# Gated linear attention: weight loads issued one stage later, and the last modulation sums made on column strips inside the last head

## The reference, cut to what matters

```python
mod_lat = jnp.split(jax.nn.silu(c) @ w_mod[layer] + b_mod[layer], N_MOD, axis=-1)
sh1, sc1, g1, sh2, sc2, g2 = mod_lat
...
q = to_heads(parts[6], GLA_HEADS)           # 4 heads, key width 128, value width 256
k = to_heads(parts[7], GLA_HEADS)
v = to_heads(parts[8], GLA_HEADS)
g_f = gla_log_gate(lr[..., :GLA_GATE_RANK], w_f, b_f)
g_b = gla_log_gate(lr[..., GLA_GATE_RANK:], w_b, b_b)
...
x = x + g1 * y_lat
h = modulate(rms_norm(x, norm_ffn_g[layer]), sh2, sc2)
```

## Time and profile before

| | |
|---|---|
| median of 3 runs | 2749.3 us (2748.82 to 2750.38) |
| the profiled execution, its own time | 2749.08 us |
| the profiled execution, its span | 2747.3 us |
| mean granted TensorE clock | 0.947 of full speed |
| busy: PE, PEld, DVE, ACT, POOL | 2458.9, 1698.2, 1244.6, 873.0, 158.3 us |
| rank stage (first transfer issued to start of the head stage) | 505.87 to 530.64 us |
| head stage (start to start of the merge) | 530.64 to 748.50 us |

### The profile page before, as it was taken

One profiled execution on the slowest core, in us unless ns is written; L12 is line 12 of the kernel. 1 busy time (PEld: TensorE's weight loads), 2 busy tenths in 40 slices (PEclk: granted clock), 3 DMA queues, 4 the chain that ended last, 5 costly groups with the idle time before them and its releaser, 6 DMA issues. The chain is left out here.

```text
span 2747.3 us, 43114 instructions
## 1 busy us (share of the span) xinstructions
PE 2458.9 (90%) x17416; PEld 1698.2 (62%) x17417; DVE 1244.6 (45%) x2882; ACT 873.0 (32%) x1889; POOL 158.3 (6%) x177
## 2 busy tenths in 40 slices
PE   6789999599799999999899988987897999888998
PEld 4667777376598443333333333326777999867998
DVE  4457776388466111111111111115756565676664
ACT  4255454223253111111111111114335355335453
POOL 0333433000000000000000000000000000000000
PEclk8889998899799999999999999998888999988999
DMA  6521210543068999999999999995313556313553
GB/s 217 72 63 40 55 33 2 163 144 126 28 197 277 397 409 409 409 409 409 409 408 409 409 409 408 409 378 176 92 36 111 163 175 178 100 54 108 173 184 114
DMA packets 254674, 601.83 MB, mean 219 GB/s; under 512 B 26146, under 2 KB 82697, under 8 KB 253449
## 3 DMA queue, kind: packets, MB, share of 16 engines
q1 hardware_dynamic: 253388, 598.58, 60.9%
q10 hardware_dynamic: 1085, 0.45, 0.1%
HBM read 594.57 MB, written 4.39 MB: 218 GB/s over the span
## 5 line engine op out<-in xcount | busy, mean ns | idle before, releaser
L2499 PE MATMUL banks<-moe_raw,moe_xs 128*64 128x512 f32 x2048 | 474.6, 601 | 30.7 <-DMA moe_raw<-in_w_gu 29.4
L2964 PE MATMUL banks<-xs_r,w_hi 128*128 128x272 f32 (+1 forms) x1408 | 408.2, 290 | 23.1 <-DVE w_raw_r L3432 14.4
L2968 PE MATMUL banks<-xs_r,w_raw_r 128*128 128x272 f32 (+1 forms) x1408 | 406.6, 289 | 0.0
L2965 PE MATMUL banks<-xs_r,w_hi 128*128 128x272 f32 (+1 forms) x1408 | 405.1, 288 | 0.0
L2499 PEld LDWEIGHTS banks<-moe_raw,moe_xs 128*64 128x64 f32 x2048 | 134.4, 137 | 301.4 <-issue 222.3
L2448 DVE TENSOR_TENSOR gu<-banks,vec 128x512 f32<-128x512 f32 x64 | 44.3, 692 | 601.8 <-PE banks L2529 601.7
L3248 ACT ACTIVATE w_hi<-w_raw 128x512 fp32r<-128x512 f32 (+1 forms) x416 | 251.6, 617 | 201.6 <-PE banks L2968 163.5
L3432 DVE TENSOR_TENSOR w_raw_r<-w_raw,w_hi 128x512 fp32r<-128x512 f32 (+1 forms) x416 | 268.1, 677 | 68.4 <-ACT w_hi L3248 64.0
L2964 PEld LDWEIGHTS banks<-xs_r,w_hi 128*128 128x128 f32 x1408 | 268.3, 191 | 27.2 <-issue 24.8
L2499 PE MATMUL banks<-moe_raw,moe_act 128*64 128x512 f32 x1024 | 240.4, 599 | 40.2 <-DMA moe_raw<-in_w_down 38.6
L2968 PEld LDWEIGHTS banks<-xs_r,w_raw_r 128*128 128x128 f32 x1408 | 268.4, 191 | 2.2
(11 more groups left out here) (508 smaller groups left out, 4096.9 us busy)
## 6 DMA issues: line engine op xcount, KB each, us to landing
moe_raw<-in_w_gu SPq DMA_DIRECT2D x256, 1024.0 KB, 18.5
moe_raw<-in_w_down SPq DMA_DIRECT2D x128, 1024.0 KB, 18.6
w_raw<-in_w_ff SPq DMA_DIRECT2D x256, 256.0 KB, 3.0
w_raw<-in_w_in SPq DMA_DIRECT2D x112, 256.0 KB, 2.7
gdn_w<-in_w_in SPq DMA_DIRECT2D x32, 512.0 KB, 4.0
mod_ring<-in_w_mod SPq DMA_DIRECT2D x16, 1024.0 KB, 5.2
ring_mod<-in_w_mod SPq DMA_DIRECT2D x8, 1024.0 KB, 18.5
wh<-in_w_in SPq DMA_DIRECT2D x8, 1024.0 KB, 9.7
```

The costliest lines, as they stand in the source:

```text
L2499: ins = pe.matmul(out if ph == "d" else out.rearrange("p (j x) -> p j x", x=P), x[:, 2 * q + k, :], w[:, c * 512:(c + 1) * 512] if ph == " ...
L2964: pe.matmul(bank, w_hi, x[:, 0, 0:n_cols], start=first, stop=False)
L2965: pe.matmul(bank, w_hi, x[:, 1, 0:n_cols], start=False, stop=False)
L2968: ins = pe.matmul(bank, w_lo, x[:, 0, 0:n_cols], start=False, stop=last)
```

## The change

Two edits, both in `gla`. First, units 0 to 2 of the modulation and the weights of head 1 are no longer issued by SP in the rank stage but as the first thing in the head stage; `load_head(0)` stays where it is. Second, the 32 products behind the last head are taken away. In their place stand, in head 3, `late_sum` behind the updates of step 0 (8 products with a weight of 32 columns, each of which writes 512 columns to one of four strips in banks 6 and 7), two copies of a bank into slot 0 of `mod_ring` by DVE at step 1, `late_turn` behind the updates of step 3 (8 products of 4 columns), and DVE's addition of the bias at step 4. There is one more semaphore.

```diff
@@ rank stage, SP
                 load_head(sp, 0)
-                for u in range(3):
-                    load_mod(sp, u)
-                load_head(sp, 1)
@@ head stage, SP
+                for u in range(3):
+                    load_mod(sp, u)
+                load_head(sp, 1)
                 late(3, 4, 5)
@@ head stage, PE
+                def late_sum():
+                    pe.wait_ge(silu_a, 2 * GLA_H)
+                    pe.wait_ge(mod_v, 8 * KT)
+                    for g in range(8):
+                        ins = pe.matmul(ps[6 + g // 4][g % 4 * Q:(g % 4 + 1) * Q, :], ones[:, 0:Q], mod_sum[:, g, :], start=True, stop=True)
+                    ins.then_inc(mod_mm, 1)
+
+                def late_turn():
+                    pe.wait_ge(mod_sb, 2)
+                    for m in range(8):
+                        ins = pe.matmul(ps[6][:, 4 * m:4 * m + 4], mod_ring[:, 0, m // 4, m % 4 * P:(m % 4 + 1) * P],
+                                        ident.rearrange("p (g q) -> p g q", g=4)[:, :, 0], start=True, stop=True)
+                    ins.then_inc(mod_mm, 1)
...
                         if h + 1 < GLA_H:
                             project(h + 1, i)
+                        elif i == 0:
+                            late_sum()
+                        elif i == 3:
+                            late_turn()
                         if h and i == 2:
                             turned(h - 1)
...
                 turned(GLA_H - 1)
-                pe.wait_ge(mod_v, 8 * KT)
-                for m in range(4 * 8):
-                    ins = pe.matmul(ps[2][:, m:m + 1], mod_sum[:, m // 4, m % 4 * P:(m % 4 + 1) * P], ones[:, 0:1],
-                                    start=True, stop=True)
-                ins.then_inc(mod_mm, 1)
@@ head stage, DVE
                         if h + 1 < GLA_H:
                             decay(h + 1, i)
+                        elif i == 1:
+                            dve.wait_ge(mod_mm, 1)
+                            for n in range(2):
+                                dve.tensor_copy(mod_ring[:, 0, n, :], ps[6 + n][:, :]).then_inc(mod_sb, 1)
+                        elif i == 4:
+                            dve.wait_ge(mod_mm, 2)
+                            dve.tensor_tensor(modT[:, 2 * KT:6 * KT, 0].rearrange("p (n g m) -> p n g m", n=2, g=4),
+                                              ps[6][:, 0:32].rearrange("p (n m g) -> p n g m", n=2, m=4),
+                                              vec[:, V_BMOD + 2 * KT:V_BMOD + 6 * KT].rearrange("p (n g m) -> p n g m", n=2, g=4), ALU.add)
                 for part in range(4):
                     norm(GLA_H - 1, part)
-                dve.wait_ge(mod_mm, 1)
-                dve.tensor_tensor(modT[:, 2 * KT:6 * KT, 0], ps[2][:, 0:4 * KT], vec[:, V_BMOD + 2 * KT:V_BMOD + 6 * KT], ALU.add)
```

More of the change, by code:

```diff
@@ L1448, in gla @@
                        "gla_cum_v gla_vv gla_diff_v gla_e_v gla_kd_v gla_att_v gla_s0 gla_s1 gla_o_v gla_sq_a gla_var_v gla_inv_v "
-                       "gla_n_v gla_y_v gla_exp_a gla_ln_a gla_ex_a gla_silu_a gla_std_a gla_mod_v gla_mod_mm", held=loaded + mod_in) as \
+                       "gla_n_v gla_y_v gla_exp_a gla_ln_a gla_ex_a gla_silu_a gla_std_a gla_mod_v gla_mod_mm gla_mod_sb", held=loaded + mod_in) as \
                 (block, gate_mm, q_mm, k_mm, v_mm, rb_mm, gram_mm, tr_mm, up0, up1, o_mm, turn_mm,
@@ L1452, in gla @@
                  cum_v, v_v, diff_v, e_v, kd_v, att_v, s0, s1, o_v, sq_a, var_v, inv_v,
-                 n_v, y_v, exp_a, ln_a, ex_a, silu_a, std_a, mod_v, mod_mm):
+                 n_v, y_v, exp_a, ln_a, ex_a, silu_a, std_a, mod_v, mod_mm, mod_sb):
             ups, ss = (up0, up1), (s0, s1)
```

## The result

| | before | after |
|---|---|---|
| median, same chip, 4 runs each | 2749.84 us (2748.82 to 2755.70) | 2732.53 us (2727.70 to 2734.74) |
| the profiled execution, its own time | 2749.08 us | 2727.70 us |
| the profiled execution, its span | 2747.3 us | 2725.9 us |

The ratio is 0.9913, 95% interval 0.9894 to 0.9932: 0.87% faster, 18.7 to 29.1 us with 23.9 in the middle. The difference of the medians is 17.3 us, that of the profiled executions 21.4. The forecast was a gain of 24.0 us and a median of 2725.3 us, with 2719 to 2735 as the range; the measured median lies in it, 7.2 us above the forecast.

A forecast was written before the change was run, and what follows sets the result against it. PE was busy 90% of the span; SP's issues held the head stage's start and 32 PE products its end. Gains of 14.75 (12.75 + 2.0) and 9.3 us sum to 24.0: 2749.3 - 24.0 = 2725.3 us, range 2719 to 2735.

The forecast's parts named there:

- What held the start: Rank stage's end: SP's issuing held it to 529.30; without seven issues DVE ends it at 516.55, 12.75 us less.
- Transfers: Head stage: all weights land in time; rival: transfers share engines evenly, about 2 to 8 us lost, chance 0.08.
- The clock at the start: Start of the head stage: with less idling PE keeps 2.4 GHz longer, 2.0 us gained (0 to 3.1).
- The last head: Head 3 and behind it: 12.76 us removed, 3.5 us of added work, so 9.3 us gained.
- The middle: From 560 to 708: PE busy 147.25 of 148 us, so what is won before is passed through.
- the clock in part: Case given 0.03 jointly with a slower kernel; a low PE clock takes part of the gain.
- From the profiled execution to the median: Whole kernel: profiled execution 0.2 us from the median of the runs; 2749.3 less 24.0 gives 2725.3 us.
- The first edit without effect: Rival at the rank stage's end: something other than SP's issuing holds it, 12.75 us not gained, 2740.0 us; chance 0.05.
- The last head eating its gain: Rival in head 3: slow `late_turn`, low clock, serial strips; 3.6 to 6.4 us instead of 9.3; chance 0.12.
- Slower by a lasting low clock: Rival: the PE-bound stretch runs at 1.2 GHz, 2778 us if through the whole head stage; 0.03 jointly with partial clock loss.
- The price of the slow clock: PE-bound head stage: 0.28 us lost per us at 1.2 GHz; the 24 us gain gone after 86 us longer.
- Six groups of products: Last three steps of the last head: 0.65 to 1.24 us each, at most 3.0 us more, 0.1 taken.

The follow-up runs named there:

- e_front: The kernel before with the first edit alone, the 32 products behind the last head kept; median 2742.04 us, ratio 0.9940.
- e_mods: The changed kernel with head 1's weights issued in the rank stage again, only units 0 to 2 moved; 2738.71 us (one run), rank stage 16.75 us.
- e_late: The changed kernel with `late_turn` behind step 7 of the last head and the bias between norm parts 2 and 3; 2732.26 us, ratio 0.9909.
- e_best2: A repeat of e_best, run beside the changed kernel; median 2728.12 us, ratio 0.9888 to the kernel before.
- e_rows: The changed kernel with gate products on 128 rows (16 to 127 zeros) and gate weights loaded behind head 0's first two transfers; 2730.89 us, ratio 0.9898.
- e_best: The changed kernel with the edits of e_rows and e_late together; median 2728.57 us, ratio 0.9885 to the kernel before.
- e_rows_before: The kernel before with only gate products on 128 rows and gate weights loaded behind head 0's first two transfers; 2753.63 us, ratio 0.9986.

## Why the prediction was right, point by point

**What held the start.** Right. With the seven issues gone the rank stage ended with DVE; the head stage's first product came 1.24 us behind DVE's copy (taken: 1.38). The rank stage lost 13.15 us in the changed kernel and 13.13 in e_front (12.75 forecast). e_mods shows the same from the other side: SP last again, the stage longer again.

**Transfers.** Head 0 was called covered "with nothing to spare" at the faster clock; its last transfer landed 9.6 us after its issue, as long as before (9.7), and missed by 0.93 us of one weight load. PE also had to wait for the first half of `z`, which DVE had at about 518.54 (half of L1613's 1.61 us behind 517.79), so the transfer cost 0.2 us at most. Units 0 and 1 and head 1 held nobody up; unit 0 landed 5.2 us after its issue, at 521.8.

**The clock at the start.** 2.0 us were taken between 0 and 3.1. From the stage's start to the key product it was 8.69 us and is 7.29: 1.4. The guess that the gates would run at 2.4 GHz and the clock fall behind them was what happened.

**The last head.** 3.5 us were taken, 3.12 measured. `late_sum` took 1.92 (1.8), so the strips do run side by side; it begins 0.64 us behind the first record of step 0, with no gap that a drain would need. The turn came 7.00 us after step 0 and not 6.24, 0.8 later (0.9). `late_turn` took 3.57 (3.4), at 1.2 GHz as assumed. e_late took 1.94 of the 3.12 away, e_best2 all of it.

**The middle.** Here one step failed: that what is won at the start is simply passed through, with nobody waiting for the clock. In 148 us between the heads PE was busy for 147.25 us before and 147.26 after, and yet it took 3.4 us longer for the same work, as it was granted 1.2 GHz at two more places. The prediction looked at the clock where it expected idleness and took it as 1.00 in between, though the trace of before already held one such dip (L1484 at 663.63 with 5.37 us). The 0.03 for "the clock in part" was too little for it: of the nine profiles with 16-row gates four have none, two or three dips instead of one, so 1.7 us less to 3.4 us more belonged to the terms of the sum, beside those of the two ends.

**From the profiled execution to the median.** The forecast took the measured scatter, 1.6 us, for the kernel's. More runs of before gave 2747 to 2767 on another chip, and even in the first comparison the fourth was 2755.7. Of the 7.2 us between forecast and median, 2.4 are between forecast and the profiled execution: the dips 3.4 and the clock at the start 0.6 on the one side, on the other 0.4 each from the last head and the rank stage and some 0.9 from ahead of the rank stage, which the change does not touch. The other 4.8 are what the median lies above that execution. For those four runs no trace says where they stand; in the pair of profiles that differ in the same way it was PE's clock behind 1856. On the other chips, with more runs, the medians of before and changed lie 23.8 us (2756.53, 2732.73) and 22.6 us (2757.02, 2734.42) apart. That the first comparison shows only 17.3, and that its median still lies in the range, says little of the forecast: with four runs each, both are in part luck.

**The rivals.** Transfers: no. The first edit without effect: no, and e_mods, where SP's issues alone make the stage longer again, shows it from the other side. The Trainium skill says (Runtime: NRT & Kernel Launch, Instruction fetch mechanics) that a branch to a target which isn't loaded forces a fetch by DMA before the engine goes on. Nothing in this trace calls for such a wait: 1.24 us at that barrier, head 0's last bytes still under way, and 1.41 at the earlier trace rows. The last head eating its gain: no, 9.6 us remained. Slower by a lasting low clock: no, but its small relative, the dips, was there.

**Where its sums and readings were off.** None of these changes the forecast. The price of the slow clock was taken as 0.28 us for each us, from 5.17 against 3.72; but that product ran from 534.36 to 539.5 and the clock was back at 537.3, so 2.2 of its 5.17 us were already fast. A dip of 3.3 us costs 1.7, that is 0.5 for each: the gain would be gone after 48 us of such a clock and not 86, and the whole head stage at 1.2 GHz would give some 2820 us and not 2778. The clock of before fell at about 520.2 (0.56 in the window from 520) and not shortly after 521. Six groups of products that grow from 0.65 to 1.24 are 3.5 us and not 3.0. Unit 0 was called covered by 4.7 us with the slow start alone; at the faster one DVE asked at 525.09, 3.3 us after it had landed. And 387 GB/s is not about all that is seen: the profile page of the kernel before has slices with 409. What a drain at a change of tiling would cost no run shows; there is no idle stretch in front of `late_sum` or behind it.

## What to carry to other kernels

An engine that issues transfers behind others still under way (here 12.5 us for four, against 1.5 for three on an almost empty queue) holds a barrier as much as one that computes: issue behind the barrier what is needed behind it, and check only that the first user is covered. Where an engine is busy all through, look at its granted clock there too: work of constant length by the timeline (here the 16 records of one product) is the best gauge of it. Work that must be done once, like eight small products, belongs in a gap that the chain leaves anyway, not ahead of a step of it.

## What the runs showed of the hardware that was not expected

PE was granted 1.2 GHz (556.8 to 560.1, for one) in the midst of work without a gap, in all 13 cases of nine profiles behind products on 16 rows of weights among updates on 64 rows; with zeros in the other 112 rows, at the same 1.96 us, this was not seen in 160 to 168 us of any of four profiles (e_rows, e_best, e_best2, e_rows_before). That zeros in those rows went with it was a surprise. Whether it is the rows alone, the rows together with the updates around them, or the changed loads and fillings of the rank stage, wasn't tried. The same program had three such stretches in two executions and one in a third, each 1.7 us.
